# Half of the first token tile's candidates searched amid the queries, and splits placed ahead of sums

## The reference

```python
def peer(xn, w_q, sub_keys, u, v):
    q = (t @ w_q).reshape(n_tok, 8, 2, 128)                 # 8 heads, 2 halves
    sc = jnp.einsum('thpd,hpnd->thpn', q, sub_keys)         # 128 keys of each half
    s1, i1 = lax.top_k(sc[:, :, 0], 16)
    s2, i2 = lax.top_k(sc[:, :, 1], 16)
    cand = (s1[..., :, None] + s2[..., None, :]).reshape(n_tok, 8, 256)
    top_s, pos = lax.top_k(cand, 16)
    eidx = jnp.take_along_axis(cidx, pos, axis=-1)          # cidx from i1, i2
    gate = jax.nn.softmax(top_s, axis=-1)
    # out[t] = sum over the chosen experts of gate * gelu(x[t] . u[e]) * v[e]
```

## Time and profile before

| | us |
|---|---|
| median of three runs | 2544.46 |
| lowest and highest | 2543.99, 2546.0 |
| the profiled execution | 2545.95 |
| its span | 2544.2 |

### The profile page before, as it was taken

One profiled execution on the slowest core, in us unless ns is written; L12 is line 12 of the kernel. 1 busy time (PEld: TensorE's weight loads), 2 busy tenths in 40 slices (PEclk: granted clock), 3 DMA queues, 4 the chain that ended last, 5 costly groups with the idle time before them and its releaser, 6 DMA issues.

```text
span 2544.2 us, 48340 instructions
## 1 busy us (share of the span) xinstructions
PE 2481.3 (98%) x17772; PEld 2283.2 (90%) x17772; DVE 1900.5 (75%) x3683; ACT 1253.4 (49%) x2078; POOL 125.9 (5%) x99
## 2 busy tenths in 40 slices
PE   8999999999999999999999999999999998999999
PEld 8999988999999889999989999998889997778999
DVE  6789996666666887889986666667877756667774
ACT  6754874444444334555854444444344445445443
POOL 0042000000000000151000000000000000000000
PEclk9999999999999999999999999999999999999999
DMA  7445677666655554455776666655545553634554
GB/s 240 142 156 176 191 208 235 211 208 205 214 191 189 189 187 170 159 173 174 203 235 211 212 211 210 207 184 188 190 142 182 176 178 109 124 112 141 181 178 156
DMA packets 192248, 467.22 MB, mean 184 GB/s; under 512 B 81618, under 2 KB 83666, under 8 KB 191200
## 3 DMA queue, kind: packets, MB, share of 16 engines
q1 hardware_dynamic: 118768, 420.52, 50.0%
q0 software_dynamic: 6992, 25.81, 3.7%
q10 hardware_dynamic: 66336, 18.88, 3.1%
HBM read 442.53 MB, written 22.61 MB: 183 GB/s over the span
## 4 chain that ended last, share of the span: by engine, by line
PE 49%; DVE 3%; ACT 1%; issue 0%; DVEq 0%; ACTq 0%
PE acc L833 14%; PE work L520 9%; PE work L521 9%; PE work L522 9%; PE acc L520 2%; PE acc L521 1%; PE acc L522 1%; PE work L847 1%; DVE ring_lo L514 1%; PE work L1062 1%; PE work L1034 1%; PE work L1046 0%; PE work L686 0%; PE work L687 0%; PE work L688 0%
## 5 line engine op out<-in xcount | busy, mean ns | idle before, releaser
L514 DVE TENSOR_TENSOR ring_lo<-ring,ring_hi 128x1024 fp32r<-128x1024 f32 (+1 forms) x759 | 924.0, 1221 | 429.9 <-ACT ring_hi L508 428.2
L508 ACT ACTIVATE ring_hi<-ring 128x1024 fp32r<-128x1024 f32 (+1 forms) x799 | 834.2, 1051 | 458.6 <-PE acc L833 372.2
L520 PE MATMUL work<-normed_hi,ring_hi 128*128 128x256 f32 (+1 forms) x2512 | 717.5, 286 | 31.2 <-DVE ring_lo L514 25.9
L521 PE MATMUL work<-normed_lo,ring_hi 128*128 128x256 f32 (+1 forms) x2512 | 711.9, 283 | 0.0
L522 PE MATMUL work<-normed_hi,ring_lo 128*128 128x256 f32 (+1 forms) x2512 | 710.0, 283 | 0.0
L833 PE MATMUL acc<-ring_hi,weighed 128*128 128x512 f32 x2048 | 589.5, 397 | 4.8 <-DVE weighed L1920 4.8
L520 PEld LDWEIGHTS work<-normed_hi,ring_hi 128*128 128x128 f32 x2512 | 476.3, 190 | 44.6 <-DVE ring_lo L514 23.2
L521 PEld LDWEIGHTS work<-normed_lo,ring_hi 128*128 128x128 f32 x2512 | 477.1, 190 | 7.9
L522 PEld LDWEIGHTS work<-normed_hi,ring_lo 128*128 128x128 f32 x2512 | 475.3, 189 | 0.0
L833 PEld LDWEIGHTS acc<-ring_hi,weighed 128*128 128x128 f32 x2048 | 374.6, 189 | 84.1 <-DVE weighed L1920 5.2
L520 PE MATMUL work<-arena_parts,ring_hi 128*128 128x256 f32 (+1 forms) x1184 | 337.7, 285 | 1.9 <-ACT arena L1135 1.1
(11 more groups left out here) (283 smaller groups left out, 2515.6 us busy)
## 6 DMA issues: line engine op xcount, KB each, us to landing
ring<-in_u SPq DMA_DIRECT2D x256, 512.0 KB, 3.3
ring<-in_v SPq DMA_DIRECT2D x256, 512.0 KB, 3.3
ring<-in_ffn_in SPq DMA_DIRECT2D x88, 512.0 KB, 3.2
ring<-in_query SPq DMA_DIRECT2D x32, 512.0 KB, 3.3
ficients_of_later_chunks<-gate_b ACTq DMA_DIRECT2D x32, 512.0 KB, 4.6
arena<-ficients_of_later_chunks POOLq DMA_DIRECT2D x32, 512.0 KB, 4.2
ring<-in_ffn_out SPq DMA_DIRECT2D x32, 512.0 KB, 4.0
ring<-in_even_in SPq DMA_DIRECT2D x28, 512.0 KB, 4.2
```

The source lines that it names most:

```text
L508: act.activation(ring_hi[:, n % RING, 0:width], ring[:, n % RING, 0:width], ACT.Copy).then_inc(hi_ready, 1)
L514: eng.tensor_tensor(ring_lo[:, n % RING, 0:width], ring[:, n % RING, 0:width], ring_hi[:, n % RING, 0:width].bitcast(F32), ALU.subtract).t ...
L520: pe.matmul(out, w_hi, hi, start=start, stop=False, **more)
L521: pe.matmul(out, w_hi, lo, start=False, stop=False, **more)
```

## The change

Four things are moved; no arithmetic is added or left out.

1. The first scores stand behind query 3 and no longer behind query 2; all others keep their place.
2. ACT's split beside the normalisation moves from k = 6 to k = 5, and VectorE's split behind the normalisation moves to k = 7 of it.
3. Sums and search of candidates become a function, `candidates(t, h0, h1)`, for heads h0 to h1 - 1. For the first token tile, heads 0 to 3 are done behind the search of group 3, heads 4 to 7 in the choice. The second tile does all eight in the choice.
4. In the choice, the split of u3 (u13) stands ahead of the cast and the sums, and the first of the two splits in the one-hot products of half x = 0 ahead of the first product rather than behind it.

```diff
@@ -140,7 +140,7 @@
-    if _j and _j % 2 == 0:
+    if _j == 3 or _j > 3 and _j % 2 == 0:
         QUERY_ITEMS += [("score", (t, _j // 2 - 1)) for t in range(NT)]
@@ -1233,7 +1233,7 @@
                     elif k in (3, 4):
                         empty(w + k - 3, query[:, k - 3, :], work[:, (w + k - 3) % 4, 0:S])
-                    elif k == 6:
+                    elif k == 5:
                         split_to(n + 2)
@@ -1774,30 +1774,39 @@
+                def candidates(t, h0, h1):
+
+                    hp = best[:, t, :, :].rearrange("p (h x) k -> p h x k", x=2)[:, h0:h1, :, :]
+                    for lo, i0, rows, width in ((0, 0, 4, TOPK), (4 * TOPK, 4, TOPK - 4, 4)):
+                        part = cand[:, h0:h1, lo:lo + rows * width].rearrange("p h (i j) -> p h i j", j=width)
+                        part_shape = [P, h1 - h0, rows, width]
+                        dve.tensor_tensor(part, hp[:, :, 0, i0:i0 + rows].unsqueeze(3).to_broadcast(part_shape),
+                                          hp[:, :, 1, 0:width].unsqueeze(2).to_broadcast(part_shape), ALU.add).then_inc(vec.sem, vec.up())
+                    step()
+                    top = pair[:, t, :].rearrange("p (h k) -> p h k", k=TOPK)
+                    at = pair_at.rearrange("p (h k) -> p h k", k=TOPK)
+                    top16(lambda r: top[:, h0 + r, :], lambda r: u32(at[:, h0 + r, :]), lambda r: cand[:, h0 + r, 0:CANDS], lambda r: cand2[:, h0 + r, 0:CANDS],
+                          h1 - h0).then_inc(vec.sem, vec.up())
...
                     step()
+                    if g == PH // 2 - 1:
+                        candidates(0, 0, PH // 2)
                 for t in range(NT):
+                    weights(u0 + (3, 13)[t])
                     dve.tensor_copy(best_f[:, t, :, :, :], u32(best_at[:, t, :, :]).rearrange("p (h x) r -> p x r h", x=2)).then_inc(vec.sem, vec.up())
...
-                    weights(u0 + (3, 13)[t])
+                    candidates(t, 0 if t else PH // 2, PH)
...
                     for x in range(2):
 
+                        if not x:
+                            weights(next(left))
                         shape = [P, TOPK, PH * TOPK // 4, 4]
...
                         step()
-                        weights(next(left))
+                        if x:
+                            weights(next(left))
                         shape = [P, TOPK, TOPK, PH]
...
             def peer(l):
                 split_to(SLOT0[f"query{l}"])
-                norm(2 * l + 1, XS, lambda k: k == 3 and split_to(SLOT0[f"query{l}"] + 1))
-                split_to(SLOT0[f"query{l}"] + 2)
+                norm(2 * l + 1, XS, lambda k: k in (3, 7) and split_to(SLOT0[f"query{l}"] + (k + 1) // 4))
```

More of the change, by code:

```diff
@@ L1782, in choose @@
                     step()
+                    if g == PH // 2 - 1:
+                        candidates(0, 0, PH // 2)
                 for t in range(NT):
+                    weights(u0 + (3, 13)[t])
                     dve.tensor_copy(best_f[:, t, :, :, :], u32(best_at[:, t, :, :]).rearrange("p (h x) r -> p x r h", x=2)).then_inc(vec.sem, vec.up())
[L1788 to L1795, removed]
-                    weights(u0 + (3, 13)[t])
+                    candidates(t, 0 if t else PH // 2, PH)
                     left = iter(range(u0 + (7, 17)[t], u0 + (13, 24)[t]))
                     top = pair[:, t, :].rearrange("p (h k) -> p h k", k=TOPK)
-                    at = pair_at.rearrange("p (h k) -> p h k", k=TOPK)
-                    top16(lambda r: top[:, r, :], lambda r: u32(at[:, r, :]), lambda r: cand[:, r, 0:CANDS], lambda r: cand2[:, r, 0:CANDS], PH).then_inc(vec.sem, vec.up())
                     step()
```

## The result

The median of five runs is 2557.72 us (2557.04 to 2560.26) against 2544.46, which stays the median of the kernel before with two more runs (five, 2543.2 to 2546.0); the ratio is 1.0055, with an interval of 1.0044 to 1.0066. The forecast was 2540.2, the range ended at 2557. The profiled execution took 2560.26 us, 2558.5 of it the span, where before it was 2544.2.

What follows compares the result with a forecast made beforehand. VectorE's chain up to L1865 was taken to set the span: -2.9 us in the first layer, -3.0 in the second, +1.6 for the clock, -4.3 in all. From the median 2544.46 that gave 2540.2 us, range 2538 to 2557.

Steps and rivals of the forecast that it cites:

- rival A: Amid the queries and in the choice, GpSimd's splits hold up VectorE's sums: 2547.0 us or more, chance 0.47 in all.
- three pieces: Sums held up: mild, 2547.0 us (chance 0.22); with the second sum, 2556.5 (0.17); in full, 2566 (0.08).
- Second form: GpSimd's next split also comes between the choice's two sums, 2 x 2.38 us more per layer: 2556.5 us, chance 0.17.
- The first search: Amid the first layer's queries, VectorE's first search starts 1.65 us later, at 149.0 us.
- One wait of 0.4 left before group 3: Amid the queries, 6.3 of VectorE's 6.7 us of waiting before searches are filled, leaving one wait of 0.4.
- The half search: Behind group 3, sums over four heads and half a search take VectorE 5.4 us.
- The choice of the first tile: VectorE's split, cast, half sums and half search take 6.86 us in place of 11.86, so -5.0 us.
- New waits of 0.7 us at u7 and u10: In the choice, VectorE, now earlier, waits for ACT's high halves of these slots, 0.7 us each.
- TensorE at query 4: TensorE waits for query 2's bank, emptied late by ACT: about 2.0 us in the first layer, 3.0 in the second.
- The clock: One drop of TensorE's granted clock behind the second layer's 3.0 us wait puts off 1.6 us of work.
- With no drop: Rival case in which the granted clock falls in neither layer: -5.9 us, 2538.6 us.

Runs made afterwards that it cites:

- reduce_input: The changed kernel with the candidates' sums replaced by a tensor_reduce over an axis of length 1 (other experts chosen): 2538.8 us.
- half_only: The kernel before with only the half search added behind group 3, first scores and all splits where they were: 2546.9 us.
- late_pool: The changed kernel with GpSimd's splits of u4 to u6 (u14 to u16) waiting until the sums of the choice are done: 2542.9 us.
- sums_first: The changed kernel with cast and sums ahead of the split of u3 (u13) again in the choice: 2546.0 us.
- pool_two: late_pool with u6 split by VectorE behind the half search, no longer by GpSimd: 2541.9 us.
- two_steps: pool_two with first scores behind query 2 again and the half search cut in two, behind groups 1 and 3: 2538.8 us.
- split_ahead: The kernel before with only the splits of u3 and u13 moved ahead of the cast and the sums: 2566.1 us.
- one_input: The changed kernel with the candidates' sums replaced by a tensor_scalar multiply of one tensor by 1 (other experts chosen): 2554.7 us.
- late_pool_old_scores: late_pool with first scores behind query 2 and the splits beside the normalisation as in the kernel before: 2543.2 us.

## Why the prediction was wrong

- **Which end of the unknown cost.** The step that failed is the choice between the forecast and rival A. The prediction said that no row shows what a split of GpSimd beside a two-tensor operation costs, and then put the sum at the end "nothing", with 0.45 against 0.47 for rival A in three pieces. What it called weak evidence (searches run undisturbed) was none: no trace shows a search held up, so they say nothing of the sums. (The prediction counts the cast with the sums as reading two tensors; it reads one, and started ahead of GpSimd's split.) The runs put 2 x 2.2 us at each pair of sums in the choice and 0.8 us amid the queries.
- **Rival A's price came close.** Second form: 1.1 + 2 x (2.2 + 2.4) = 10.3 us per layer, less 1.3 that VectorE's other waits take in, 2556.5 with no drop of the clock and 2558.1 with the one forecast. Measured 0.8 + 4.4 + 4.4 = 9.6 per layer; from `reduce_input` (-2.6, -2.8) to the change (+5.6, +8.0) it is 8.2 and 10.8, the latter with 1.7 of clock; 2557.7. The range ended at 2557.0, 0.7 below.
- **The first search** was to start at 149.0 and did at 149.32 in a trace that ran 0.27 us late there. Right. One wait of 0.4 left before group 3: 0.49. Right in the first layer; in the second the fall of the clock made scores late and two more waits (0.67, 1.40).
- **The half search** 5.4 us: with nothing held up 0.7 + 4.8 = 5.5 (171.19 to 176.67 in `reduce_input`). Right.
- **The choice of the first tile, -5.0 us**: right for splits, sums and search, but the list left out what stands behind the search. GpSimd's 7.1 us had needed all of a 9.2 us search as cover. Neither the forecast nor rival A priced the copy that is now exposed: 2.2 us in `half_only` and `late_pool`, 1.4 in `reduce_input`.
- **New waits of 0.7 us at u7 and u10**: not seen in the change (the held-up sums make VectorE the late one), 2.9 at u7 in `sums_first` (1.3 of it clock), 0.8 and 0.3 at u10 and u11 in `sums_first`, `pool_two` and `two_steps`, none in `reduce_input`. The mechanism is right, and its size hangs on when TensorE gets u3, the coupling that makes the half search alone worth 0.1 and 0.4 us.
- **TensorE at query 4**: 2.0 and 3.0 us forecast, 1.58 and 2.58 measured; both 0.4 too large.
- **The clock**: one drop of 1.6 us in the second layer, measured 1.7 in the change, but in five of eight traces none behind the same wait. That it came in the change is luck. The drop behind the 1.79 us wait at u3, which was put at 0.7 us and free, was not foreseen. With no drop the forecast was 2538.6, and `reduce_input` is 2538.8, closer than its runs lie together (2536.8 to 2541.0).

So where nothing holds up the sums the moves do about what they were reckoned to do, and the one cost that was set to nothing was larger than all of them: 8.2 and 10.8 us per layer, from `reduce_input` to the change, against a gain of 2.6 and 2.8.

## What to carry to other kernels

Where a change puts an operation beside work on GpSimd that it never stood beside, and no row prices the pair, take the blocked duration as the likelier end until a run says otherwise, and ask which kind of operation it is rather than how many tensors it reads. Work that is hidden under another operation has a length: who shortens the cover must look at what comes out at its end. And an engine that waits for a ring may be waiting for itself, so time saved ahead of its own feeding step comes back as a wait a few slots later.

## What the runs showed of the hardware

- A GpSimd subtraction of 128x1024 (2.38 us) held up each of VectorE's two sums by 2.2 us, and the two engines took turns instruction by instruction; with instructions a quarter as long the hold-up was 0.55 us each.
- Held up: `tensor_tensor` of float32, `tensor_scalar` of one tensor, and a copy of 128x8 (0.17 to 2.4 us). Not held up: maxima, places and replacements (half a search takes 4.9 us with one split of 2.4 us beside it, from 204.26 us in the change, and with most of three, from 199.65 us in `reduce_input`) and `tensor_reduce` (0.69 us beside a split). A cast that began 0.16 us ahead of GpSimd's split ran in 0.37 us.
- GpSimd in its turn is held up a little: three splits of 7.12 us took 7.97.
- Within each of TensorE's six waits of 5.8 us (two in the change, four in `split_ahead`) and two of 5.3 (`one_input`) the granted clock fell to 0.50, and it stayed down past their ends, where 1.7 to 2.9 us of work were put off. Behind waits of 1.7 to 2.8 us it fell in some traces and not in others: behind that of 2.58 us in three of eight, behind 2.72 and 2.77 us in none of two in `half_only` and both of 2.77 in `sums_first`, behind 1.74 us in `late_pool_old_scores` and not in `pool_two`. Each fall put off 1.7 us of work.
